# A two-block transformer kernel: the context's projections and attention computed beside the experts, and the experts' second matrices in one buffer, requested by ScalarE

## The chip, the cores and the metric

The kernel runs on one core of one Trainium2 chip. The metric is the device time of one execution in microseconds (us); the time of a kernel is the median of its runs.

## The reference

All data is float32. The input has 512 tokens (D = 1024) and, for the second block, 256 context tokens. The first block is a mixer with two kinds of attention, a layer of 32 experts (two per token) and a gated side input. The second block has two layers; in its first (grouped attention, 16 query heads on 4 key heads of 64) context tokens are queries too:

```python
def hier_moe(x, ...):                      # per expert e, on the tokens routed to it
    hdn = silu(xb @ w1[e]) * (xb @ w3[e])  # w1, w3: 1024 x 512
    return hdn @ w2[e]                     # w2: 512 x 1024, 2 MB each

def gqa_mixer(h, hc, p, cos, sin, with_ctx_out):
    k, v, q, g = split(h @ w_in, ...)      # w_in: 1024 x (256 k, 256 v, 1024 q, 1024 g)
    proj_c = hc @ w_in                     # context: k, v, q, g as well
    k_all, v_all = concat([kc, k]), concat([vc, v])
    o = attend(q, k_all, v_all)            # 512 queries over 768 keys
    y = (o * silu(g)) @ w_out
    oc = attend(qc, kc, vc)                # 256 context queries over the 256 context keys
    yc = (oc * silu(gc)) @ w_out
```

`hc` is the normalised and modulated context. It depends on the inputs alone, not on the first block. q and k are normalised per head and, for the 512 tokens, rotated.

## The kernel before

The program has two blocks, `first_layer` and `second_layers`, with a barrier between them. The rows of a tensor lie on 128 partitions, so the 512 tokens are tiles t = 0 to 3 and the context is tiles 4 and 5. Each engine has its own list of instructions in an order written out by hand; semaphores (`s[...]`) tie them together. An engine that waits holds up everything behind it on its list. DMAs are asked for by SyncE (`sp`), mostly; each engine that asks has a queue of its own.

**The experts.** A loop over e = 0 to 30 (`STATIC` = 31) is unrolled. Every expert takes at most 64 tokens; a loop with a number of passes known only at run time (the "over" loop) does expert 31 and whatever exceeds 64. For each expert PE computes, in this order: the first product of e (`first_product(p1, w1b[p])`), the transposes of the hidden rows of e - 1 (`hidden`), the third matrix's product of e, the transposes of the next expert's rows (`turn_rows`), and the second product of e - 1 (`second`). ScalarE applies silu (L1175) and evicts the second product, scaled by the gates (`outputs`, L1169); VectorE multiplies and copies; GpSimd gathers rows and scatters results. Each of the three matrices (2 MB) has two buffers, used in turn. SyncE asks for them in the order w1, w3, w2 of expert e; it waits for w1's buffer on `h1`, for w3's on `h3`, and for w2's on `y`, the second product of e - 2. Beside the experts PE, ScalarE and VectorE do small jobs at fixed values of e: the modulation rows, tables, the lists for the over loop, and, at e = 20 to 29, the norm of the side input and of the context, whose transposed and modulated tiles are `ctx_in`. At the end of the block SyncE asks for the first six pieces (1 MB each) of `l0_w_in`.

**The second layers.** PE's list begins with the projection of the context (units `("c", n, t)`: three chunks of 512 columns, two tiles, 8 products each), then the context's gates (`("cg", j)`), transposes of `hx` (`("p", t)`) that wait for the sum with the experts' output `y`, the side gate, and the projections of the tokens. All large products are recorded on L1872, transposes on L1880. The attention (`class Attention`, object `gqa`) goes over 8 pairs of heads; for each it has a list of units (pair, tile, first key tile, last key tile, output group, column). Per step n PE computes the scores of unit n + 1 (L327) in one PSUM buffer, the transposes of the next pair's queries and keys if due (L312, `turn_step`), the transposes of the weights of unit n (L339), and the values of unit n - 1 (L353). VectorE takes the maximum (L443), ScalarE the exponential (L526). After it come the output products and the second layer with its own attention (`mla`) of the same class.

## Time and profile before

| | us |
|---|---|
| three timed runs | 2036.48, 2024.63, 2036.65 |
| their median | 2036.48 |
| the profiled execution | 2025.51 |
| its span, first to last instruction | 2023.7 |
| PE busy | 1790.9 (88%) |
| VectorE busy | 732.0 (36%) |
| ScalarE busy | 521.1 (26%) |
| granted TensorE clock, mean | 0.97 |
| bytes moved by DMA | 333.45 MB |

The profile is of one execution. Durations of matmuls are modelled at their ends, so that a busy PE isn't PE at its peak; a product of float32 with 512 columns is recorded as two instructions. The share of busy time is an average over stages with different limits, so a stage has to be read by itself.

### The profile page before, as it was taken

The page shows a single profiled execution, that of the slowest core. Times are in us where ns is not written, and L with a number is a line of the kernel's source. Part 1 is how long each engine was busy: PE and PEld are TensorE (multiplying, and loading weights), DVE is VectorE, ACT ScalarE, POOL GpSimd, SP SyncE. Part 2 cuts the span into 40 slices and gives each one's busy share as a digit, 9 for nine tenths or more (in the row PEclk, how much of TensorE's full clock was granted, in tenths as well). Part 3 has the DMA queues.
Part 4 walks back from the last instruction along what each step waited for, and adds up shares of the span by engine and source line. Part 5 has one row for each costly group of instructions (what it writes and reads, how often), then busy time and mean ns, then how long its engine had stood idle before and what let it go on. Part 6 is the DMA issues. An engine that isn't in the chain of part 4 may idle for free.

```text
span 2023.7 us, 24040 instructions
## 1 busy us (share of the span) xinstructions
PE 1790.9 (88%) x9628; PEld 1007.5 (50%) x9628; DVE 732.0 (36%) x1432; ACT 521.1 (26%) x1102; POOL 152.0 (8%) x202
## 2 busy tenths in 40 slices
PE   8999878978887778875999998888998999699998
PEld 3333455544444444443564445666545544467663
DVE  2333675231131111121213264666333225555542
ACT  2111575210000001110223123445211233234330
POOL 2110000001111111111000130000000000100000
PEclk9999999989999899998999999999998999899999
DMA  7655946269999999998522220000200011000001
GB/s 264 216 182 182 161 73 132 111 259 384 421 421 420 420 421 421 421 420 359 207 85 83 83 83 1 1 1 1 97 0 31 21 57 63 21 1 1 1 22 42
DMA packets 91951, 333.45 MB, mean 165 GB/s; under 512 B 10112, under 2 KB 26624, under 8 KB 64832
## 3 DMA queue, kind: packets, MB, share of 16 engines
q1 hardware_dynamic: 81536, 310.56, 42.1%
q0 software_dynamic: 5200, 17.04, 2.1%
q10 hardware_dynamic: 5104, 4.30, 0.7%
q8 instruction: 77, 1.26, 0.3%
q14 instruction: 34, 0.28, 0.1%
HBM read 317.58 MB, written 14.30 MB: 164 GB/s over the span
## 4 chain that ended last, share of the span: by engine, by line
PE 42%; ACT 6%; DVE 2%; issue 2%; POOL 1%; ACTq 0%; DVEq 0%; POOLq 0%
PE tail_ps L1872 27%; PE tail_ps L327 7%; ACT arena L526 5%; PE tail_ps L339 3%; PE tail_ps L353 2%; PE tail_ps L312 1%; PE tail_ps L1880 1%; POOL extra L2409 1%; DVE tail_small L443 0%; PE tail_ps L373 0%; DVE arena L2368 0%; DVE side L208 0%; DVE arena L208 0%; DVE arena L2369 0%; ACT arena L208 0%
## 5 line engine op out<-in xcount | busy, mean ns | idle before, releaser
L1000 PE MATMUL mix_ps<-arena 128*64 128x256 f32 x2048 | 253.5, 404 | 94.4 <-issue 60.9
L1000 PEld LDWEIGHTS mix_ps<-arena 128*64 128x64 f32 x2048 | 163.1, 145 | 183.6 <-issue 88.9
L1872 PE MATMUL tail_ps<-arena 128*128 128x512 f32 x504 | 219.7, 592 | 0.1
L443 DVE TENSOR_REDUCE tail_small<-tail_ps 128x1 f32<-128x768 f32 (+1 forms) x160 | 128.7, 846 | 150.8 <-PE tail_ps L327 150.8
L888 PE MATMUL mix_ps<-arena,side 128*128 128x512 f32 x384 | 175.5, 610 | 1.4 <-DVE side L1217 1.4
L1872 PEld LDWEIGHTS tail_ps<-arena 128*128 128x128 f32 x504 | 95.1, 190 | 115.2 <-issue 114.7
L526 ACT ACTIVATE arena<-tail_ps,tail_small 128x768 f32<-128x768 f32 (+1 forms) x160 | 128.6, 813 | 3.7 <-DVE tail_small L443 3.7
L888 PEld LDWEIGHTS mix_ps<-arena,side 128*128 128x128 f32 x384 | 72.3, 194 | 103.6 <-issue 85.4
L1872 PE MATMUL tail_ps<-arena,side 128*128 128x512 f32 (+2 forms) x320 | 122.1, 543 | 0.0
L1012 PE MATMUL mix_ps<-arena 128*64 128x512 f32 x512 | 116.9, 598 | 2.3 <-issue 1.8
L339 PE MATMUL tail_ps<-first,arena 128*128 128x128 f32 x832 | 107.3, 277 | 1.2 <-ACT arena L526 0.4
L339 PEld LDWEIGHTS tail_ps<-first,arena 128*128 128x128 f32 x832 | 92.3, 141 | 19.5 <-issue 16.0
L327 PE MATMUL tail_ps<-side,arena 96*128 96x512 f32 (+1 forms) x256 | 92.1, 503 | 8.8 <-ACT arena L526 8.1
L1399 DVE COPY arena<-mix_ps 128x256 f32<-128x256 f32 x31 | 13.2, 424 | 220.3 <-PE mix_ps L1005 219.6
L1169 ACT ACTIVATE arena<-mix_ps,mix_small 128x512 f32<-128x512 f32 x31 | 21.3, 687 | 274.5 <-PE mix_ps L1012 274.5
L1872 PEld LDWEIGHTS tail_ps<-arena,side 128*128 128x128 f32 x320 | 62.3, 196 | 57.1 <-issue 45.4
L327 PE MATMUL tail_ps<-side 64*128 64x256 f32 (+1 forms) x320 | 61.2, 492 | 27.7 <-ACT arena L526 26.6
L1872 PE MATMUL tail_ps<-side,arena 128*128 128x512 f32 x192 | 83.9, 592 | 0.0
L327 PEld LDWEIGHTS tail_ps<-side,arena 96*128 96x128 f32 x256 | 46.5, 191 | 48.8 <-issue 35.2
L1872 PE MATMUL tail_ps<-arena,extra 128*128 128x512 f32 (+1 forms) x128 | 51.3, 561 | 16.1 <-PEq L164 16.1
L1012 PEld LDWEIGHTS mix_ps<-arena 128*64 128x64 f32 x512 | 34.4, 136 | 60.8 <-issue 57.3
L1574 POOL DMA_INDIRECT expert_out<-arena,mix_indices x31 | 30.6, 987 | 424.5 <-ACT arena L1169 417.4
(344 smaller groups left out, 2178.6 us busy)
## 6 DMA issues: line engine op xcount, KB each, us to landing
arena<-in_w SPq DMA_DIRECT2D x96, 2048.0 KB, 18.1
arena<-in_l_w_in SPq DMA_DIRECT2D x22, 1024.0 KB, 7.4
arena<-in_l_w_mod SPq DMA_DIRECT2D x16, 1024.0 KB, 5.0
arena<-in_w_in SPq DMA_DIRECT2D x12, 1024.0 KB, 9.3
arena<-in_l_w_mod SPq DMA_DIRECT2D x16, 512.0 KB, 4.6
residual<-bias_blocks SPq DMA_DIRECT2D x32, 224.0 KB, 13.0
arena<-in_l_w_out SPq DMA_DIRECT2D x6, 1024.0 KB, 5.2
arena<-in_w_out SPq DMA_DIRECT2D x4, 1024.0 KB, 14.7
```

The costliest lines, as they stand in the source:

```text
L312: ins = pe.transpose(Tp[0:rows, bank, z * P:(z + 1) * P], src, m["ident"])
L327: ins = pe.matmul(self.scores_of(n, x)[:, a * P:e * P], q, k, start=True, stop=True)
L339: ins = pe.transpose(Tp[:, bank, z * P:(z + 1) * P], pr[:, n % self.PRB, x, kt * P:(kt + 1) * P], m["ident"])
L353: ins = pe.matmul(O[x * self.dv:(x + 1) * self.dv, oc * P:(oc + 1) * P], self.value_of(g, x, lo + kt), weight, start=(kt == 0), stop=(kt = ...
L443: dve.tensor_reduce(nm[:, b, x:x + 1], self.scores_of(n, x), AX.X, ALU.max, negate=True).then_inc(s["maxed"], 1)
L526: act.activation(pr[:, b, x, 0:k], in_, ACT.Exp, bias=nm[:, b, x:x + 1], scale=scale, accum_out=sm[:, og_b, z, x:x + 1]).then_inc(s["exped ...
L888: last = pe.matmul(ps[:, u % 4], oT[:, k, t * P:(t + 1) * P], weights.slot(W_IN[n, k // 4], 4, 512)[:, k % 4], start=(k == 0), stop=(k == ...
L1000: last = pe.matmul(out[h * CAP:(h + 1) * CAP, 0:H2], x, wb[:, k, h * H2:(h + 1) * H2], start=(k == 0), stop=(k == DK - 1))
L1012: last = pe.matmul(py[h * CAP:(h + 1) * CAP, :], x, wb[:, f, h * 512:(h + 1) * 512], start=(f == 0), stop=(f == FK - 1))
L1169: act.activation(yb[:, e % 2], py, ACT.Copy, scale=gate_w[:, e:e + 1]).then_inc(s["y_out"], 1)
L1574: pool.indirect_dma_start(out=y_rows, out_offset=bass.IndirectOffsetOnAxis(ap=index[:, 1, e:e + 1], axis=0), in_=yb[:, e % 2], in_offset=N ...
L1872: last = pe.matmul(out, lhs(k), rhs(k), start=(k == 0), stop=(k == K - 1))
```

## The change

It has three parts.

1. **The second matrices.** w2 has one buffer, `w2b`. SyncE asks for that of expert 0; ScalarE asks for the one of expert e on its own queue, right after it has evicted the second product of e - 1. In the over loop SyncE waits for all 31 second products before it asks.
2. **The context beside the experts.** The norms at e = 20 to 29 move to e = 1 to 11. At e = 12 to 23 PE does one half unit of the context's k, v, q projection per expert (`context_product`, four products of 512 columns), with weights that come in six pieces of 1 MB into one buffer, asked for by SyncE between the experts' matrices. ScalarE copies the results out and squares them, VectorE normalises (e = 15 to 25). From e = 24 (`C_FIRST`) on, three steps per expert (`context_step`) compute the attention of the 256 context queries over the 256 context keys, in 16 units of two heads by one tile; the buffers lie in SBUF that w2's second buffer and the lists had.
3. **The second layers.** The three chunks `("c", ...)` are gone and the gates come first; the `gqa` object has four units per pair instead of six; the context's gate is multiplied by VectorE (`gate_context`); norms and rotations cover the four token tiles alone.

```diff
-    w2b = [view(proj_w, 8192, D_EXPERT // P, D), view(work, 4096, D_EXPERT // P, D)]
+    w2b = view(proj_w, 8192, D_EXPERT // P, D)
...
-            expert(0, "w2")
-            expert(1, "w2")
+            sp.dma_start(runs(w2b), A["w2"][0].rearrange("(a p j) n -> p a (j n)", a=2, p=P)).then_inc(s["w2"], 16)
...
             for e in range(2, STATIC):
-                for which in ("w1", "w3", "w2"):
-                    expert(e, which)
-                if e == 14:
-                    sp.wait_ge(s["over_indexed"], 1)
+                expert(e, "w1")
+                if e == 2:
+                    sp.wait_ge(s["side_ev"], 2 * XT)
                     sp.dma_start(side_gain, A["g_ple"]).then_inc(s["side_gain"], 16)
+                expert(e, "w3")
+                if e in range(13, 25, 2):
+
+                    i = (e - 13) // 2
+                    sp.wait_ge(*((s["c_mm"], 2 * i) if i else (s["over_indexed"], 1)))
+                    sp.dma_start(piece, src_c[:, 4 * (i % 2):4 * (i % 2) + 4, 512 * (i // 2):512 * (i // 2 + 1)]).then_inc(s["c_in"], 16)
             sp.wait_ge(s["over_indexed"], 1)
             p = STATIC % 2
             with sp.Fori(0, sp.value_load(trips_over, min_val=1, max_val=OVER + 1)) as i:
                 e = sp.value_load(experts_over[:, ds(i, 1)], min_val=0, max_val=N_EXPERTS - 1)
...
+            for n, free in enumerate(("h1", "h3")):
...
-                pe.wait_ge(s["w2"][e % 2], 16 * (e // 2 + 1))
...
+                pe.wait_ge(s["w2"], 16 * (e + 1))
...
+            def context_product(i):
+
+                n, z, t = i // 4, i // 2 % 2, i % 2
+                pe.wait_ge(s["c_in"], 16 * (i // 2 + 1))
+                if i == 0:
+                    pe.wait_ge(s["ctx_gained"], 2)
+                if z == 0 and n:
+                    pe.wait_ge(s["c_ev"], 2 * (n - 1) + t + 1)
+                for k in range(4):
+                    last = pe.matmul(ps[:, 5 + t], ctx_in[:, t, 4 * z + k], piece[:, k], start=(z == 0 and k == 0), stop=(z == 1 and k == 3))
+                last.then_inc(s["c_mm"], 1)
+
+            def context_step(i):
+
+                u, v, w = i - 2, i - 3, (i - 5) // 2
+                if 0 <= u < C_UNITS:
+                    p, t = u // 2, u % 2
+                    pe.wait_ge(s["qk_taken"], qk_after(p))
+                    pe.wait_ge(*((s["ctx_exped"], 2 * u) if u else (s["c_ev"], 6)))
+                    for x in range(2):
+                        last = pe.matmul(ps[:, 5, 256 * x:256 * (x + 1)], qTc[p % 2][:, x, t * P:(t + 1) * P], kTc[p // 2 % 2], start=True, stop=True)
+                    last.then_inc(s["ctx_scored"], 1)
+                if i % 2 == 0 and i < C_UNITS:
+                    p = i // 2
+                    pe.wait_ge(s["c_normed"], 6 if p < 4 else 9)
+                    pe.wait_ge(s["c_ev"], 6)
+                    if p >= 3:
+
+                        pe.wait_ge(s["ctx_o"], p - 2)
+                    if p:
+                        pe.wait_ge(s["qk_taken"], qk_after(p - 1))
+                    for t in range(2):
+                        for x in range(2):
+                            last = pe.transpose(ps[0:64, 6, x * CTX + t * P:x * CTX + (t + 1) * P], cproj[:, t, 512 + p * P + 64 * x:576 + p * P + 64 * x], m["ident"])
+                    if p % 2 == 0:
+                        for t in range(2):
+                            last = pe.matmul(ps[64:128, 6, t * P:(t + 1) * P], cproj[:, t, 32 * p:32 * p + 64], m["ident"], start=True, stop=True)
+                    last.then_inc(s["qk_turned"], 1)
+                if i % 2 and 0 <= w < 8:
+                    pe.wait_ge(s["ctx_taken"], 2 * w + 2)
+                    pe.wait_ge(s["qk_taken"], qk_after(min(w + 2, 7)))
+                    g = w // 2
+                    for t in range(2):
+                        for kt in range(2):
+                            for x in range(2):
+                                last = pe.matmul(ps[64 * x:64 * x + 64, 6, t * P:(t + 1) * P], cproj[:, kt, 256 + 64 * g:256 + 64 * (g + 1)],
+                                                 pTc[t][:, 2 * x + kt], start=(kt == 0), stop=(kt == 1))
+                    last.then_inc(s["ctx_pv"], 1)
+                if 0 <= v < C_UNITS:
+                    pe.wait_ge(s["ctx_scaled"], v + 1)
+                    pe.wait_ge(*((s["ctx_taken"], v) if v else (s["over_indexed"], 1)))
+                    for x in range(2):
+                        for kt in range(2):
+                            last = pe.transpose(ps[:, 7, (2 * x + kt) * P:(2 * x + kt + 1) * P], pr_c[:, v % 2, x, kt * P:(kt + 1) * P], m["ident"])
+                    last.then_inc(s["ctx_weights"], 1)
...
+                if e >= C_FIRST:
+                    context_step(3 * (e - C_FIRST))
                 pe.wait_ge(s["w3"][p], 16 * (e // 2 + 1))
                 if e:
                     pe.wait_ge(s["hid"], e)
@@ -1045,21 +1118,26 @@
                 if e + 1 < STATIC:
 
                     turn_rows(xg[:, 1 - p], s["got"][1 - p], 16 * ((e + 1) // 2 + 1), s["xg_turned"])
+                if e >= C_FIRST:
+                    context_step(3 * (e - C_FIRST) + 1)
                 if e:
                     second(e - 1)
+                if e >= C_FIRST:
+                    context_step(3 * (e - C_FIRST) + 2)
+                if e in range(12, 24):
+                    context_product(e - 12)
...
+            def take_context(i):
+
+                n, t = i // 2, i % 2
+                H = 4 if n == 0 else 8
+                act.wait_ge(s["c_mm"], 4 * n + t + 3)
+                act.activation(cproj[:, t, 512 * n:512 * (n + 1)], ps[:, 5 + t], ACT.Copy).then_inc(s["c_ev"], 1)
+                act.wait_ge(s["c_ev"], i + 1)
+                if i:
+                    act.wait_ge(s["c_normed"], 3 * n + 1 if t else 3 * n - 1)
+                act.activation(sq_c[:, 0:64 * H], cproj[:, t, 512 * n:512 * n + 64 * H], ACT.Square).then_inc(s["own_squared"], 1)
+
+            def context_step(i):
+                u = i - 2
+                if 0 <= u < C_UNITS:
+                    act.wait_ge(s["ctx_maxed"], u + 1)
+                    if u >= 2:
+                        act.wait_ge(s["ctx_weights"], u - 1)
+                    for x in range(2):
+                        act.activation(pr_c[:, u % 2, x], ps[:, 5, 256 * x:256 * (x + 1)], ACT.Exp, bias=nm_c[:, u % 2, x:x + 1], scale=1.0,
+                                       accum_out=sm_c[:, u % 2, x:x + 1]).then_inc(s["ctx_exped"], 1)
+                if i % 2 == 0 and i < C_UNITS:
+                    p = i // 2
+                    act.wait_ge(s["qk_turned"], p + 1)
+                    act.activation(qTc[p % 2], ps[0:64, 6].rearrange("p (x q) -> p x q", x=2), ACT.Copy).then_inc(s["qk_taken"], 1)
+                    if p % 2 == 0:
+                        act.activation(kTc[p // 2 % 2], ps[64:128, 6, 0:256], ACT.Copy).then_inc(s["qk_taken"], 1)
...
-                    act.wait_ge(s["over_indexed"], 1)
-                if e in range(20, 24):
-                    if e > 20:
-                        act.wait_ge(s["own_squared"], e - 20)
-                    act.activation(own, view(side, 0, XT, D)[:, e - 20], ACT.Square, accum_out=ss_s[:, e - 20:e - 19]).then_inc(s["own_squared"], 1)
-                if e in (24, 25):
+                    act.dma_start(w2b.rearrange("p (a j) n -> p a (j n)", a=2), A["w2"][e].rearrange("(a p j) n -> p a (j n)", a=2, p=P)).then_inc(s["w2"], 16)
+                if e >= C_FIRST:
+                    context_step(3 * (e - C_FIRST) + 2)
...
+            def context_step(i):
+                u, v, w = i - 2, i - 3, (i - 5) // 2
+                if 0 <= u < C_UNITS:
+                    dve.wait_ge(s["ctx_scored"], u + 1)
+                    dve.tensor_reduce(nm_c[:, u % 2], ps[:, 5].rearrange("p (x k) -> p x k", x=2), AX.X, ALU.max, negate=True).then_inc(s["ctx_maxed"], 1)
+                if i % 2 and 0 <= w < 8:
+                    dve.wait_ge(s["ctx_pv"], w + 1)
+
+                    dve.tensor_copy(cproj[:, :, 512 + w * P:512 + (w + 1) * P], ps[:, 6, 0:256].rearrange("p (t q) -> p t q", t=CT)).then_inc(s["ctx_o"], 1)
+                if 0 <= v < C_UNITS:
+                    dve.wait_ge(s["ctx_weights"], v + 1)
+                    if v >= 2:
+                        dve.wait_ge(s["ctx_pv"], v // 2)
+                    dve.tensor_copy(pTc[v % 2].rearrange("p k q -> p (k q)"), ps[:, 7]).then_inc(s["ctx_taken"], 1)
+                if 0 <= u < C_UNITS:
+                    dve.wait_ge(s["ctx_exped"], 2 * u + 2)
+                    chain(dve.reciprocal(rc_c[:, u % 2], sm_c[:, u % 2]))
+                    dve.tensor_tensor(pr_c[:, u % 2], pr_c[:, u % 2], rc_c[:, u % 2].unsqueeze(2).to_broadcast([P, 2, CTX]), ALU.mult).then_inc(s["ctx_scaled"], 1)
...
-        pieces = [(q_of[a:e], P, [qT[:, p % 2, a * P:e * P]]) for a, e in ((0, 4), (4, AT))]
+        pieces = [(q_of[0:XT], P, [qT[:, p % 2, 0:XT * P]])]
...
-                    [(p, t, 0, AT, 2 * p, t) if t < XT else (p, t, XT, AT, 2 * p + 1, t - XT) for p in range(8) for t in range(AT)], 2, 1,
+                    [(p, t, 0, AT, p, t) for p in range(8) for t in range(XT)], 2, 1,
...
-            for n in range(3):
-                arrived("c", n)
-                for t in (4, 5):
-                    product(start(("c", n, t)), lambda k: hcT[:, t - 4, k], weights_of(2 * n), range(DK)).then_inc(s["mm"], 1)
             for j in range(DK):
                 if j % 4 == 0:
                     arrived("cg", j // 4)
                 product(start(("cg", j))[:, 0:CTX], lambda k: weights_of(2 * (j // 4))(k)[:, j % 4 * P:(j % 4 + 1) * P], lambda k: hcT[:, :, k], range(DK)).then_inc(s["mm"], 1)
-                if j < XT:
-                    pe.wait_ge(s["added_y"], j + 1)
-                    turn(("p", j), cut(hx[:, j]), DK)
+                t = {3: 0, 4: 1, 6: 2, 7: 3}.get(j)
+                if t is not None:
+                    pe.wait_ge(s["added_y"], t + 1)
+                    turn(("p", t), cut(hx[:, t]), DK)
...
+            def gate_context(j):
+
+                dve.wait_ge(*emptied(("cg", j)))
+                dve.tensor_tensor(gT_c[:, j].rearrange("p (t q) -> p t q", t=CT), gT_c[:, j].rearrange("p (t q) -> p t q", t=CT),
+                                  proj[:, XT:AT, 512 + j * P:512 + (j + 1) * P], ALU.mult).then_inc(s["gated_c"], 1)
```

## Rows read from the trace of the kernel before

**Rows 1.** The page's slices of 50.6 us: tenths of the DMA engines' time.
```profile
DMA  7655946269999999998522220000200011000001
```

**Rows 2.** Windows: stretch, length, busy PE, PEld, DVE, ACT, POOL; clock, DMA share, GB/s.
```profile
450.00:460.00 10.00, 10.00 (x74) 5.29 (x72) 2.81 (x12) 0.69 (x1) 1.11 (x2) 1.00 0.45 154
...
500.00:900.00 400.00, 317.30 (x2134) 177.03 (x2132) 66.69 (x170) 37.85 (x67) 48.94 (x50) 0.96 1.01 420
```

**Rows 3.** Timeline of PE, one expert: start, busy us, what, idle time before.
```profile
702.49 5.32 PE L1000 MATMUL mix_ps<-arena 128*64 128x256 f32 x32 [2.55 <-issue]
...
712.46 3.65 PE L1012 MATMUL mix_ps<-arena 128*64 128x512 f32 x16
```

**Rows 4.** Timeline of ScalarE: evictions of the second product, seven experts apart.
```profile
813.31 0.69 ACT L1169 ACTIVATE arena<-mix_ps,mix_small 128x512 f32<-128x512 f32 x1 [9.57 <-PE mix_ps L1012]
...
926.80 0.69 ACT L1169 ACTIVATE arena<-mix_ps,mix_small 128x512 f32<-128x512 f32 x1 [8.58 <-PE mix_ps L1012]
```

**Rows 5.** Timeline of PE, two successive first products while weights lay ready.
```profile
445.60 3.67 PE L1000 MATMUL mix_ps<-arena 128*64 128x256 f32 x32 [0.78 <-DVE arena L1392]
...
458.09 3.67 PE L1000 MATMUL mix_ps<-arena 128*64 128x256 f32 x32
```

**Rows 6.** Groups by line, PE, 961 to 1010 us: busy, mean ns, idle before.
```profile
L1872 PE MATMUL tail_ps<-arena,extra 128*128 128x512 f32 x96 | 43.2, 613 | 16.1 <-PEq L164 16.1
```

**Rows 7.** Chain that ended last, gqa attention: start, us, what.
```profile
1235.43 1.58 PE tail_ps L327 x8
...
1261.03 1.56 PE tail_ps L327 x8
...
1265.69 1.56 PE tail_ps L327 x8
...
1270.35 1.56 PE tail_ps L327 x8
...
1288.31 1.56 PE tail_ps L327 x8
...
1314.27 1.56 PE tail_ps L327 x8
...
1449.03 41.44 PE tail_ps L1872 x96
```

**Rows 8.** Timeline of the same attention: a short unit's operations on three engines.
```profile
1258.06 0.76 DVE L443 TENSOR_REDUCE tail_small<-tail_ps 128x1 f32<-128x256 f32 x2 [1.17 <-PE tail_ps L327]
...
1258.68 0.60 PE L339 MATMUL tail_ps<-first,arena 128*128 128x128 f32 x4
...
1259.21 1.53 PE L353 MATMUL tail_ps<-arena 128*64 128x128 f32 x24
...
1259.87 0.47 ACT L526 ACTIVATE arena<-tail_ps,tail_small 128x256 f32<-128x256 f32 x1
```

**Rows 9.** Chain that ended last, the second layer's attention (mla).
```profile
1777.16 2.85 PE tail_ps L327 x8
...
1782.95 2.85 PE tail_ps L327 x8
...
1789.11 2.36 PE tail_ps L327 x6
...
1816.33 2.36 PE tail_ps L327 x6
```

**Rows 10.** DMA issues: source, queue, count, KB each, median us to landing.
```profile
arena<-in_l_w_out SPq DMA_DIRECT2D x6, 1024.0 KB, 5.2
```

**Rows 11.** DMA issues of the first 30 us, ScalarE's queue, in order of issue.
```profile
params<-in_params ACTq DMA_DIRECT2D x1, 439.0 KB, 6.7
...
consts<-in_consts ACTq DMA_DIRECT2D x1, 1181.5 KB, 10.9
```

**Rows 12.** Timeline of ScalarE's queue at the start.
```profile
7.86 0.46 ACTq L1099 DMA_DIRECT2D consts<-in_consts  x1
```

**Rows 13.** Window, columns as in rows 2.
```profile
10.00:15.00 5.00, 5.00 (x15) 2.53 (x14) 0.00 (x0) 0.00 (x0) 0.00 (x0) 1.00 1.04 410
```

203 lines of the change are left out of this document (116 added, 87 removed).

## The prediction

> **What bounds the kernel now.** I read the page's slices first: the DMA engines are at nine tenths from about 450 to 950 us and nearly idle afterwards [rows 1]. So there are two regimes, the experts and the second layers, and a move from one to the other has a different price in each. The windows put it in numbers: from 500 to 900 us the DMA share is 1.01 at 420 GB/s, while PE is busy for 317 of 400 us [rows 2]. The timeline of one expert shows who waits: PE is idle for 2.55 us, then needs 5.32 us for the first product, and later 3.65 us for the product with the second matrix [rows 3]. Evictions seven experts apart are 113.5 us apart [rows 4]: a cycle of 16.2 us. Where the weights already lay in SBUF, the same first product took 3.67 us and two starts were 12.49 us apart, a small turn of modulation rows (0.6) among it [rows 5]: PE needs 11.9 us per expert. The cycle is that of the weights, and PE has 16.2 - 11.9 = 4.3 us of cover in each. From 961 us on PE is the chain: the context's three projection chunks take 96 instructions at its head [rows 6], and the stretch from the first scores of the second layer's attention (1235.43) to the output products (1449.03) is 213.6 us [rows 7], a loop of scores, maximum and exponential.
>
> **Removed from the tail: the projections.** Six units of 8 products, 96 instructions. They were busy 43.2 us [rows 6]; the same count runs in 41.44 us elsewhere [rows 7], and the slow first few will now fall on the gate products. That is -41.4 us, all on PE's own chain. The turns of hx, which wait for the sums of y, move behind gate products 3, 4, 6 and 7, and so keep gate products ahead of them where the projections were; I expect 0 to 3 us of waiting, taken as 0.
>
> **Removed from the tail: context queries.** Before, a pair of heads has 4 units over 768 keys and 2 over 256. Scores of full units are 4.66 us apart (1261.03, 1265.69, 1270.35); the first full units of three pairs in a row start at 1261.03, 1288.31 and 1314.27: 27.3 us for a pair beside which keys are turned too, 26.0 without [rows 7]. Now there are 32 full units: 32 x 4.66 = 149.1 us. The turn of the next pair no longer lies beside short units but in the third full one. A turn of queries alone puts four transposes (0.6 us [rows 8]) ahead of the weights that ScalarE must empty before its exponential: 0.5 us, four times. With keys it is 1.3 more (27.3 against 26.0): 1.8 us, three times. Together 7.4, and 4.5 for the last unit's weights, values and division, which are exposed. 161.0 against 213.6 is -52.6 us; the last unit is now a long one, later by 1: -51.6. Bounds: turns at nothing, -60; turns as in the other attention, whose pairs have four units with six pieces to turn and start 27.22 us apart, where its units alone, 5.79 apart, would take 23.2 [rows 9], so 4 us each: -31. One piece or three are nearer to my figure than to six.
>
> **Added to the experts: the pieces.** Six loads of 1.05 MB, 6.29 MB at 420 GB/s [rows 2]: +15.0 us, because here nothing hides a byte. At the end of the stage the old loads of these weights cost nothing: they landed behind the barrier. Bounds: 0 (if the stage had idle DMA time where they fall) and 15. SyncE waits for a product before it asks for the next piece; queued behind that wait is the first matrix of an expert whose buffer isn't free sooner anyway.
>
> **Added: twelve products of four, experts 12 to 23.** 8 instructions of 0.43 us (41.44 / 96 [rows 7]), 3.45 us each. The cycle there is 16.2 + 1.25 = 17.4 us by DMA; PE needs 11.9 + 3.45 = 15.4, and 17.0 with the slow first product of [rows 3]. Nothing; if that cover is gone, up to 0.8 us x 12 = 10.
>
> **Added: the context's attention, experts 24 to 30.** On PE: 16 scores; both heads now lie on partitions 0 to 63, so I take the unpacked price, a third (256 of 768 columns) of the 2.85 us of the other attention's scores [rows 9], 0.95 each: 15.2. Sixteen times four transposes at 0.6, 9.6; eight value products of 16 instructions at 1.1 (24 take 1.53), 8.8; eight query turns at 0.6 and four key turns at 0.5, 6.8 [rows 8]. Together 40.4 us. Seven cycles took 113.5 us; free-running PE would take 7 x 11.9 = 83.3, so 30.2 are cover and +10.2 us stick out. Stalls: from the scores of a step to the transposes of its weights lie one expert product (3.6) and some 3 us of the step's own work, 6.7 us. The chain in between is scores 0.95, maximum 0.8, two exponentials 1.0 with their sums [rows 8], inverse and scaling some 0.9, and gaps: about 4.5. Taken as covered. Bounds: 0 to +33 for all of it.
>
> **Moved: the second matrices.** Before, SyncE asks for them when the product two experts back has read them, and its wait on that product also holds back the first and third matrices behind it. Now ScalarE asks once the product just before is evicted, into the one buffer. The loop is: product 3.65, eviction 0.76 with its wait [rows 3, 4], transfer. In a cycle of 16.2 this leaves 11.8 us. A lone 1 MB lands 5.2 us after its issue [rows 10], so 2.7 us are fixed and 2.1 MB need 7.7. Beside a full SyncE queue ScalarE's share is visible once, at the start: 439 and 1181.5 KB on its queue, the second issued at 7.86 us and landed 10.9 later [rows 11, 12], at 18.8, while the engines moved 410 GB/s [rows 13]. From the first one's issue, 0.4 us earlier, that is 11.3 us for 1.66 MB; less 2 us fixed, 178 GB/s. At this throughout, 2.1 MB need 11.8, the loop 3.65 + 0.76 + 2.7 + 11.8 = 18.9 us. But then SyncE's queue would run dry for 2.7 us in each cycle, as it has only 4.2 MB there and two buffers for each; its dry time falls into the transfer, which then has all engines. With some 7 of 9 us contended it fits the 16.2. I take +0.3 us in ten cycles ahead of the pieces, +3, nothing later, where cycles are longer. At the start the wait on y no longer blocks the fourth expert's matrices: of the 5.5 us of idle DMA between 450 and 460 us [rows 2] I take back 1, since one second matrix is no longer loaded ahead: +2 in sum, bounds -5 and +53 (18.9 in every cycle: 2.7 x 10 + 1.5 x 12 + 1.2 x 7).
>
> The Trainium skill ("DMA: Bandwidth & Descriptors", Queues, rings and completion order) says that each DMA engine goes round the queues that have work, a packet at a time. Halves of 420 would give 10.0 us of transfer and a loop of 17.1, where the one row that shows a share gives 18.9 (178 of 410 is 43%); the sum above needs neither. Its page "Trainium Kernel Development and Optimization" (Best Practices) says to double-buffer so that DMA overlaps compute, and this change takes a buffer away; by that rule the cycle would be the loop's, which is the first rival below.
>
> Everything else (norms, squares, the gate multiplication on DVE) is on engines that are mostly idle; that the context rows' output products start before the attention's end shortens nothing, since PE is dense there.
>
> **Sum** against the profiled run, 2025.5 us (span 2023.7): -41.4 - 51.6 + 15.0 + 10.2 + 2 = -65.8, so 1959.7. Two of the three timed runs lie 11 us above the profiled one, one does not; for a median I add half of that: 1965.
>
> **Rivals.**
> 1. *The one buffer sets the cycle.* For it: 178 GB/s in the only row with two full queues. Against: SyncE can't keep the engines full in a longer cycle. At one more us in 22 cycles, 1987; at 18.9 everywhere, 2016. Chance 0.12.
> 2. *It does so with three queues.* GpSimd's gathers and scatters share the engines too. If ScalarE gets a third, 140 GB/s, the transfer takes 15.0 us and the loop 22.1: 5.9 x 10 + 4.7 x 12 + 4.4 x 7 = 146 us, 2109: slower. It decides from a loop of about 19.6 us (a share of 168 GB/s in every cycle), which eats the whole gain. Against: the gathers are 0.5 MB in a cycle. Chance 0.03.
> 3. *PE stands in the context steps.* PE waits in order for two other engines, each bound to its own order around the expert. 1.5 us in each of 20 steps is +30: 1995. For it: ScalarE must alternate between exponentials and the experts' function; against: the 2.2 us of margin above. Chance 0.13.
> 4. *Turns as dear as in the other attention*: 1986. Chance 0.10.
> 5. *It doesn't add what I count*: pieces and steps fill idle time: 1940. Chance 0.05.
> My own sum, 0.57, with a range of 1948 to 1982.
>
> Range 1938 to 2000: it leaves out rival 2, the far half of 1 and parts of 3. A difference of 1% (20 us) is what a measurement here can tell from none. Faster by over 1% (under 2016): all but rival 2 and the end of rival 1, 0.93; same 0.03; slower 0.04.
>
> **What would show it.** The wait that PE had ahead of the first product moves ahead of the second matrix's; cycles are 16.2 to 16.5 us before expert 12, 17.4 to 23, 17.5 to 18 afterwards. Rival 1 shows 17.2 or more before expert 12 and a DMA share under 0.97 there. Rival 3 shows PE idle inside the steps. In the tail: gates as the first products, attention in 161 us, pairs about 19.7 us apart. I would be wrong above all where a cycle of experts 2 to 11 isn't the DMA engines' any more.

## The result and the profile after

The changed kernel takes 2014.63 us (median of 20 runs, 2006.88 to 2025.43), the one before 2029.43 us (20 runs, 2024.63 to 2036.65). The ratio is 0.9927 (95% interval 0.9913 to 0.9940): 15 us faster, where 66 were forecast. The time lies outside the range (1938 to 2000, with 1965 as the forecast), and in the class to which the forecast gave 0.03.

The profiled executions are 2020.8 us (span 2018.7) and 2025.5 us (span 2023.7). ScalarE's evictions of the second product y(e) cut both at the same places. In the changed kernel (timeline of ScalarE, first, 11th, 23rd, 30th and 31st eviction):

```profile
468.93 0.69 ACT L1247 ACTIVATE arena<-mix_ps,mix_small 128x512 f32<-128x512 f32 x1 [7.92 <-PE mix_ps L1027]
...
644.21 0.69 ACT L1247 ACTIVATE arena<-mix_ps,mix_small 128x512 f32<-128x512 f32 x1 [6.88 <-PE mix_ps L1027]
...
868.76 0.69 ACT L1247 ACTIVATE arena<-mix_ps,mix_small 128x512 f32<-128x512 f32 x1 [13.44 <-PE mix_ps L1027]
...
996.38 0.69 ACT L1247 ACTIVATE arena<-mix_ps,mix_small 128x512 f32<-128x512 f32 x1 [8.40 <-PE mix_ps L1027]
...
1009.95 0.69 ACT L1247 ACTIVATE arena<-mix_ps,mix_small 128x512 f32<-128x512 f32 x1 [12.89 <-PE mix_ps L1027]
```

| stretch | before | after | difference | forecast |
|---|---|---|---|---|
| start to y(0) | 457.6 | 468.9 | +11.3 | 0 |
| y(0) to y(10) | 158.5 | 175.3 | +16.8 | +2 |
| y(10) to y(22), pieces and products | 197.2 | 224.5 | +27.3 | +15 |
| y(22) to y(29), steps | 113.5 | 127.6 | +14.1 | +10.2 |
| y(29) to y(30) | 4.7 | 13.6 | +8.9 | 0 |
| over block and barrier | 30.3 | 29.3 | -0.9 | 0 |
| second part to the attention's first scores | 273.7 | 233.4 | -40.3 | -41.4 |
| attention to the output products | 213.6 | 171.3 | -42.3 | -51.6 |
| rest | 574.7 | 574.7 | 0 | 0 |

The sum is -5.0, up to rounding. The 11.3 us at the start lie in code that the change doesn't touch (the granted clock from 400 to 430 us was 0.77, against 0.93 before; the last section shows two executions of one code that differ by as much); without them it is -16.3, which fits the medians' -14.8. So the tail gave nearly what was forecast, and the experts cost 67 us in place of 27.

The page's groups (before, then changed) say where PE waits: ahead of the second product now, where it had waited ahead of the first product. They also say that the second product itself got slower, 145.2 us for the same 512 instructions where it had been 116.9.

```profile
L1000 PE MATMUL mix_ps<-arena 128*64 128x256 f32 x2048 | 253.5, 404 | 94.4 <-issue 60.9
...
L1012 PE MATMUL mix_ps<-arena 128*64 128x512 f32 x512 | 116.9, 598 | 2.3 <-issue 1.8
```
```profile
L1015 PE MATMUL mix_ps<-arena 128*64 128x256 f32 x2048 | 238.1, 386 | 2.5 <-DVE arena L1510 2.5
...
L1027 PE MATMUL mix_ps<-arena 128*64 128x512 f32 x512 | 145.2, 719 | 66.9 <-DMA arena<-in_w 66.3
```

Two cycles in a row, in the timeline, and the same two as windows (columns as in [rows 2]):

```profile
504.31 0.38 ACTq L1300 DMA_DIRECT2D arena<-in_w  x1
...
519.64 5.34 PE L1027 MATMUL mix_ps<-arena 128*64 128x512 f32 x16 [6.48 <-DMA arena<-in_w]
...
525.04 0.37 ACTq L1300 DMA_DIRECT2D arena<-in_w  x1
...
534.29 3.65 PE L1027 MATMUL mix_ps<-arena 128*64 128x512 f32 x16
...
538.00 0.37 ACTq L1300 DMA_DIRECT2D arena<-in_w  x1
```

```profile
480.00:920.00 440.00, 382.98 (x2314) 192.18 (x2316) 97.49 (x240) 64.79 (x119) 47.60 (x48) 0.91 0.98 395
504.30:525.00 20.70, 14.22 (x91) 7.11 (x91) 2.91 (x11) 2.11 (x4) 1.96 (x2) 0.84 1.00 416
525.00:538.00 13.00, 13.00 (x89) 6.68 (x90) 2.23 (x4) 2.12 (x5) 1.96 (x2) 1.00 0.93 355
```

The DMA issues of those two stretches, with the time to landing:

```profile
arena<-in_w ACTq DMA_DIRECT2D x1, 2048.0 KB, 15.3
arena<-in_w ACTq DMA_DIRECT2D x1, 2048.0 KB, 8.6
```

Up to y(10) the cycles alternate. In the long one w2 lands 15.3 us after its request and PE stands 6.48 us for it. In the short one it lands after 8.6 us, but PE needs 13.0 us for its own work and can't be any faster. At the start of the short cycle the four buffers of w1 and w3 are full, so SyncE has nothing to ask for until PE has read one, and the DMA engines fall to 355 GB/s over the cycle. These two cycles make 16.9 us on average, the ten from y(0) to y(10) 17.5, where the cycle before was 16.2.

The long cycle is long for a second reason: the clock. The second product as windows, in the long cycle and in the short one:

```profile
519.64:524.98 5.34, 5.33 (x17) 1.50 (x17) 0.00 (x0) 0.00 (x0) 0.00 (x0) 0.68 0.97 403
534.29:537.94 3.65, 3.65 (x18) 1.12 (x17) 0.69 (x1) 0.00 (x0) 0.00 (x0) 1.00 1.00 422
```

Behind the wait of 6.48 us the granted clock was 0.68 in the mean of the product, so in part at 1.2 GHz, the lower of the two levels, and the product took 5.34 us. Where PE hadn't waited it stayed at 2.4 GHz and took 3.65. The next w2 is asked for only behind this product, so what it loses goes round the loop. In the five long cycles up to y(10) it took 5.99, 5.34, 5.59, 5.09 and 6.60 us, in the short ones 3.65: 10.4 of the 16.8 us that this stretch lost.

And the last second matrix is asked for behind y(29), at 996.38 us, with nothing left to cover it:

```profile
1004.79 5.11 PE L1027 MATMUL mix_ps<-arena 128*64 128x512 f32 x16 [8.03 <-DMA arena<-in_w]
```

### The profile page after: what moved, and what is told of

Same layout as the page of the kernel before. It is cut to its first block and busy times, and to the rows that moved or that the text cites. A ratio compares the mean times of both kernels' runs of the same rounds, so it can differ in the third digit from the quotient of the medians.

```text
span 2018.7 us, 24057 instructions
## 1 busy us (share of the span) xinstructions
PE 1821.2 (90%) x9644; PEld 1007.6 (50%) x9644; DVE 753.6 (37%) x1471; ACT 540.1 (27%) x1110; POOL 148.2 (7%) x194
## 5 line engine op out<-in xcount | busy, mean ns | idle before, releaser
L1015 PE MATMUL mix_ps<-arena 128*64 128x256 f32 x2048 | 238.1, 386 | 2.5 <-DVE arena L1510 2.5
L1027 PE MATMUL mix_ps<-arena 128*64 128x512 f32 x512 | 145.2, 719 | 66.9 <-DMA arena<-in_w 66.3
L1015 PEld LDWEIGHTS mix_ps<-arena 128*64 128x64 f32 x2048 | 143.3, 138 | 89.1 <-issue 20.2
L903 PE MATMUL mix_ps<-arena,side 128*128 128x512 f32 x384 | 175.3, 609 | 1.4 <-DVE side L1335 1.4
L443 DVE TENSOR_REDUCE tail_small<-tail_ps 128x1 f32<-128x768 f32 x128 | 116.6, 953 | 137.7 <-PE tail_ps L327 137.7
L526 ACT ACTIVATE arena<-tail_ps,tail_small 128x768 f32<-128x768 f32 x128 | 113.8, 899 | 3.7 <-DVE tail_small L443 3.7
L1027 PEld LDWEIGHTS mix_ps<-arena 128*64 128x64 f32 x512 | 40.6, 164 | 147.6 <-issue 77.2
L339 PE MATMUL tail_ps<-first,arena 128*128 128x128 f32 x768 | 98.2, 277 | 9.5 <-DVE side L208 8.3
L339 PEld LDWEIGHTS tail_ps<-first,arena 128*128 128x128 f32 x768 | 85.9, 142 | 24.5 <-issue 15.8
L2031 PEld LDWEIGHTS tail_ps<-side,arena 128*128 128x128 f32 x192 | 36.5, 190 | 45.9 <-issue 45.9
L2031 PE MATMUL tail_ps<-extra,arena 128*128 128x256 f32 (+1 forms) x160 | 45.7, 444 | 15.1 <-PEq L164 15.1
## 6 DMA issues: line engine op xcount, KB each, us to landing
residual<-bias_blocks SPq DMA_DIRECT2D x32, 224.0 KB, 10.1
```

Of the source, the lines that this page charges most:

```text
L339: ins = pe.transpose(Tp[:, bank, z * P:(z + 1) * P], pr[:, n % self.PRB, x, kt * P:(kt + 1) * P], m["ident"])
L443: dve.tensor_reduce(nm[:, b, x:x + 1], self.scores_of(n, x), AX.X, ALU.max, negate=True).then_inc(s["maxed"], 1)
L526: act.activation(pr[:, b, x, 0:k], in_, ACT.Exp, bias=nm[:, b, x:x + 1], scale=scale, accum_out=sm[:, og_b, z, x:x + 1]).then_inc(s["exped ...
L903: last = pe.matmul(ps[:, u % 4], oT[:, k, t * P:(t + 1) * P], weights.slot(W_IN[n, k // 4], 4, 512)[:, k % 4], start=(k == 0), stop=(k == ...
L1015: last = pe.matmul(out[h * CAP:(h + 1) * CAP, 0:H2], x, wb[:, k, h * H2:(h + 1) * H2], start=(k == 0), stop=(k == DK - 1))
L1027: last = pe.matmul(py[h * CAP:(h + 1) * CAP, :], x, wb[:, f, h * 512:(h + 1) * 512], start=(f == 0), stop=(f == FK - 1))
```

## The experiments

All ratios are to the kernel before. The stretches are read from each run's profile, by the same evictions as above, in us.

| kernel | ratio (95%) | y(0)-y(10) | y(10)-y(22) | y(22)-y(29) | y(29)-y(30) | y(0)-y(30) |
|---|---|---|---|---|---|---|
| before | 1 | 158.5 | 197.2 | 113.5 | 4.7 | 473.8 |
| one_sp | 1.0059 (1.0034-1.0084) | 160.9 | 196.6 | 113.2 | 14.0 | 484.7 |
| two_act | 0.9989 (0.9972-1.0005) | 153.3 | 199.1 | 109.7 | 8.7 | 470.9 |
| one_act | 1.0280 (1.0234-1.0326) | 177.1 | 212.1 | 121.4 | 18.5 | 529.1 |
| act_held_2 | 1.0332 (1.0288-1.0375) | 184.4 | 219.4 | 129.8 | 19.7 | 553.3 |
| after | 0.9927 (0.9913-0.9940) | 175.3 | 224.5 | 127.6 | 13.6 | 541.0 |
| after_sp | 1.0159 (1.0131-1.0186) | 161.2 | 283.9 | 127.6 | 14.7 | 587.4 |
| after_sp_piece | 0.9788 (0.9748-0.9829) | 161.3 | 211.2 | 127.6 | 14.8 | 514.9 |
| no_steps | 0.9895 (0.9852-0.9938) | 176.4 | 223.4 | 119.1 | 14.8 | 533.7 |
| ring5 | 0.9819 (0.9777-0.9861) | 155.5 | 238.5 | 127.6 | 4.6 | 526.3 |
| ring5_piece | 0.9731 (0.9691-0.9770) | 154.6 | 212.7 | 127.6 | 4.6 | 499.6 |
| spread | 0.9652 (0.9620-0.9684) | 155.8 | 211.5 | 115.0 | 5.5 | 487.8 |
| spread_turn | 0.9627 (0.9602-0.9652) | 155.7 | 211.8 | 115.0 | 5.5 | 487.9 |

**The second matrices in the kernel before: buffer and queue apart.** one_act does the change's first part alone.

```
-    w2 of expert e: SyncE, behind w1(e), w3(e), into w2b[e % 2] when y >= e - 1
+    outputs(e - 1)
+    act.dma_start(w2b[0], A["w2"][e]).then_inc(s["w2"], 16)
```

> The kernel before with one part of the change alone: a single buffer for the second matrices, which ScalarE requests on its own queue behind each eviction of y. Theory 1, the one buffer costs: the matrix can be asked for only at y(e-1) and for part of each second cycle nothing is left to move, so the 30 cycles take 17.2 to 17.5 us in place of 16.2 (+30 to +40 us) and the last matrix lies bare at the end (+5 to +9 us): ratio 1.017 to 1.024. Theory 2, not the buffer but the second queue: the same time here. Theory 3, the products and attention steps beside the experts cost what is missing, the buffer nothing: ratio 1.00 to 1.005.

one_sp has the one buffer and keeps SyncE's queue; the loop asks in the order of use.

```
-    for which in ("w1", "w3", "w2"): expert(e, which)
+    expert(e, "w1"); expert(e, "w3")
+    sp.wait_ge(s["y"], e - 1); sp.dma_start(w2b[0], A["w2"][e - 1])
```

> The kernel before with the single buffer, but the second matrices stay on SyncE's queue, asked for in the order of use (w1(e), w3(e), w2(e-1)). Theory 1 (the buffer): as dear as with ScalarE's queue, 1.015 to 1.03, since the matrix can be asked for no earlier and the next first matrix now stands behind it. Theory 2 (two queues share the engines badly): the cycles are back at 16.2 us and only the last matrix at the end costs, ratio 1.00 to 1.005. Theory 3: 1.00.

two_act has both buffers and ScalarE's queue.

```
     outputs(e - 1)
+    act.dma_start(w2b[(e + 1) % 2], A["w2"][e + 1])
```

> The other half of the change to the second matrices alone: the kernel before with both its buffers, but ScalarE asks for w2(e+1) on its own queue behind the eviction of y(e-1), the moment at which the buffer comes free. Theory A (the loss needs both, one buffer and a transfer that shares the engines with matrices needed later): with a whole expert of slack the slow landing of w2 (12 to 15 us) is hidden, ratio 0.995 to 1.005. Theory B (two queues as such waste the engines): 1.01 to 1.03.

The windows of the three, one_sp, two_act, one_act:

```profile
480.00:920.00 440.00, 340.67 (x2358) 189.21 (x2360) 74.04 (x189) 39.69 (x71) 52.81 (x54) 0.99 1.01 420
```
```profile
480.00:920.00 440.00, 363.31 (x2392) 196.63 (x2390) 76.33 (x190) 40.34 (x72) 51.91 (x53) 0.91 1.01 421
```
```profile
480.00:920.00 440.00, 342.87 (x2189) 172.89 (x2191) 66.48 (x182) 36.02 (x66) 48.95 (x50) 0.88 0.97 390
```

One buffer alone leaves the transfers at 420 GB/s and costs 11 us, of which 9.3 are the bare last matrix; the ratio, 1.0059, lies just above theory 2's range. The second queue alone leaves them at 421 and costs nothing. Together they cost 55 us, more than theory 1 had expected, and the rate falls to 390. Neither "the one buffer" nor "two queues as such" holds: it takes both.

act_held and act_held_2 asked whether it is the order: in one_act SyncE asks for w1(e + 2) 8 to 19 us ahead of w2(e) (from 500 to 540 us). The edit, as act_held_2 has it:

```
                 if e >= 2:
                     sp.wait_ge(s[dict(w1="h1", w3="h3")[which]], e - 1)
+                    if e > 2:
+                        sp.wait_ge(s["y_out"], e - 2)
```

> As one_act (the kernel before, one buffer, second matrices on ScalarE's queue), but SyncE holds w1(e) and w3(e) back until y(e-2) is evicted, the moment at which ScalarE asks for w2(e-1): still two queues and one buffer, but the matrices that are needed later are no longer asked for first. Theory A, the order: w2 shares the engines with matrices asked for 8 us earlier and needed an expert later; held back, the 30 cycles fall from 17.6 us to 16.2 to 16.5 and the ratio from 1.028 to 1.006 to 1.012. Theory B, two queues as such waste the engines: the ratio stays at 1.02 to 1.03. Theory C, holding back starves the queue: over 1.03.

act_held had `y_out >= e - 1` as its only wait, one expert too long. Ratio 1.1784, DMA share 0.60: the starved queue of theory C, which says nothing on the order.

> act_held with its hold set right: w1(e) and w3(e) are now held back until y(e-3) is evicted, as SyncE's own order in one_sp had them (act_held held them one expert longer and starved the queue, which says nothing of the order). Theory A: w2(e-2) and w1(e), w3(e) are asked for at the same moment, no later matrix is ahead of the second one; the 30 cycles fall from 17.6 us to 16.2 to 16.7, ratio 1.006 to 1.012 in place of 1.028. Theory B: 1.02 or more.

It came out at 1.0332, not at 1.006 to 1.012: theory A in this form is wrong. one_sp and act_held_2 ask for the same matrices at nearly the same moments, and differ in the queue of w2. The landing of w2, for three requests of one_sp (at 594, 643 and 659 us) and four in a row of act_held_2 (from 701 us on):

```profile
arena<-in_w SPq DMA_DIRECT2D x1, 2048.0 KB, 12.5
arena<-in_w SPq DMA_DIRECT2D x1, 2048.0 KB, 12.4
arena<-in_w SPq DMA_DIRECT2D x1, 2048.0 KB, 12.9
```
```profile
arena<-in_w ACTq DMA_DIRECT2D x1, 2048.0 KB, 11.5
arena<-in_w ACTq DMA_DIRECT2D x1, 2048.0 KB, 15.7
arena<-in_w ACTq DMA_DIRECT2D x1, 2048.0 KB, 11.1
arena<-in_w ACTq DMA_DIRECT2D x1, 2048.0 KB, 16.4
```

Behind what SyncE had asked for before and ahead of what it asks for next, w2 lands in 12.4 to 12.9 us each time, and 12.4 + 3.65 is the cycle of 16.2. On a queue of its own it shares the engines with whatever SyncE's queue then holds, and its landing swings between 11 and 16. With two buffers a late landing has an expert of slack; with one it is PE's time at once, and in the changed kernel an early one isn't paid back, as PE has 12 to 13 us of its own work in a cycle. The Trainium skill ("DMA: Bandwidth & Descriptors", Queues, rings and completion order) says that SP and ACT each own one row of queues and that an engine goes round the rows for which it has work; the landings agree, while no run here shows the packets themselves. The Trainium skill ("Trainium Kernel Development and Optimization", Best Practices) also says to double-buffer; one_sp shows that rule broken for 1.5 us in the 29 cycles to y(29), with the transfers at 420 GB/s all the while, and for 9.3 us in the last one.

The swing isn't the whole joint cost; most of it is the clock behind the waits. The group of the second product in one_act, one_sp and after_sp_piece (below):

```profile
L1016 PE MATMUL mix_ps<-arena 128*64 128x512 f32 x512 | 159.2, 779 | 127.6 <-DMA arena<-in_w 126.9 <-issue 0.7
```
```profile
L1018 PE MATMUL mix_ps<-arena 128*64 128x512 f32 x512 | 123.3, 625 | 53.2 <-DMA arena<-in_w 53.2
```
```profile
L1032 PE MATMUL mix_ps<-arena 128*64 128x512 f32 x512 | 124.3, 630 | 28.9 <-DMA arena<-in_w 26.3 <-issue 2.5
```

In one_sp PE stands for w2 as well, but mostly for some 1.6 us at a time, and from 480 to 920 us the granted clock is 0.99; in one_act it is 0.88. So of the 44.4 us between one_act and one_sp from y(0) to y(30) some 36 are second products that ran slower behind a longer wait. act_held_2 (161.2 us in this group) shows both terms side by side, as PE waits for w2 in each of its 30 cycles: their mean of 18.4 us is 13.3 from the request to the product and 5.1 of product, where one_sp has 12.3 (in the 28 in which it waits) and 3.8. In two_act the granted clock falls too (0.91), but there the waits and the slow products are the first ones (6.19 us at 659.12, behind a wait of 6.41), the second is busy for 118.5 us in all, and w2, with its second buffer, is in time all the same. No run holds the clock, so what the swing of the landings would cost at 2.4 GHz is not shown.

**The same in the changed kernel.** after_sp is the changed kernel with one_sp's order of requests.

```
     expert(e, "w1"); expert(e, "w3")
+    sp.wait_ge(s["y"], e - 1); sp.dma_start(w2b, A["w2"][e - 1])
     if e in range(13, 25, 2): ... sp.dma_start(piece, ...)
```

> The changed kernel with its one buffer, but the second matrices asked for by SyncE in the order of use (w1(e), w3(e), w2(e-1)); all else as changed. Theory A or B (ScalarE's queue costs, by order or as such): evictions of y(0) to y(10) come within 161 us in place of 175, the stretch of y(10) to y(22) falls from 224.5 to 205 to 215 us, y(29) to y(30) stays at 14 us; ratio 0.975 to 0.985. Theory of the one buffer (already weakened): no change, 0.993.

The first stretch did as theory A or B said (161.2), but the second rose to 283.9. A piece now stood behind w2(e - 1) and its wait for y, and so was asked for an expert after its buffer had been read:

```profile
731.50 0.47 SPq L857 DMA_DIRECT2D arena<-in_l_w_in  x1
...
744.85 6.56 PE L1060 MATMUL mix_ps<-arena,extra 128*128 128x512 f32 x8 [13.80 <-DMA arena<-in_l_w_in]
```

In the changed kernel, where SyncE doesn't wait for y, PE stood for no piece: its waits from 644 to 869 us are all for w2. after_sp_piece puts the piece in its own place in the order of use, ahead of w1(e).

```
+    if e in range(13, 25, 2): ... sp.dma_start(piece, ...)
     expert(e, "w1")
     expert(e, "w3")
     sp.wait_ge(s["y"], e - 1); sp.dma_start(w2b, A["w2"][e - 1])
-    if e in range(13, 25, 2): ... sp.dma_start(piece, ...)
```

> The changed kernel with its one buffer for the second matrices, asked for by SyncE in the order of use (as after_sp), and with the pieces of context's projection asked for ahead of w1(e), in their place in the order of use, too (as ring5_piece). after_sp alone fell to 1.016, because a piece now stood behind a request that waits for y and TensorE then stood 13.8 us for it. If the joint cost of one buffer and a second queue is what the forecast missed in the changed kernel as in the one before: y(0) to y(10) 161 us, y(10) to y(22) 210 to 216 (224.5 as changed), y(22) to y(29) 127.6 unchanged (TensorE sets it), y(29) to y(30) 13 to 15; ratio 0.978 to 0.985 in place of 0.993. If in the changed kernel another cost is hidden behind it: over 0.99.

All four stretches and the ratio are within what was expected. From y(0) to y(30) it is 26.1 us under the changed kernel: that is the joint cost there. The second product's group fell from 145.2 to 124.3 us, so some 21 of the 26.1 stand in it. What is left over the kernel before is 2.8 and 10.1 us for the one buffer (first and last stretch), 14.0 for the pieces and 14.1 for the steps.

**Five buffers that any matrix may use.** ring5 keeps the changed kernel's SBUF, but SyncE asks for all 93 matrices in the order of use, number i into buffer i % 5.

```
+    turn_of: w1(e) -> 3e - 1, w3(e) -> 3e, w2(e) -> 3e + 4
+    i = turn_of(which, e); _, of, before = order_of_use[i - 5]
+    sp.wait_ge(s[dict(w1="h1", w3="h3", w2="y")[of]], before + 1)
+    sp.dma_start(five[i % 5], A[which][e]).then_inc(s["five"][i % 5], 16)
```

> The changed kernel with the same five buffers, but any matrix may lie in any of them: SyncE asks for all 93 matrices in the order of use, each into the buffer that was freed five matrices earlier; ScalarE asks for none. Theory 1: queue never runs dry, cycles of experts 0 to 12 are back at 16.2 us (-13 us), those with pieces at 17.4 (-16 us), and the last matrix is covered (-6 to -9 us): ratio to the kernel before 0.975 to 0.982. Theory 2 (one queue in place of two) gives the same here. Theory 3 (PE's added work sets the cycles from expert 12 on): -13 us at most before expert 12, -9 at the end, ratio 0.983 to 0.987.

The ratio is as theory 1 had it, but not by its stretches: the first is back under that of before (155.5), the last as before (4.6), yet the second rose by 14 us. A piece again stands behind four matrices that are needed later:

```profile
619.01 0.47 SPq L857 DMA_DIRECT2D arena<-in_l_w_in  x1
...
645.78 6.64 PE L1060 MATMUL mix_ps<-arena,extra 128*128 128x512 f32 x8 [13.56 <-DMA arena<-in_l_w_in]
```

ring5_piece moves the pieces ahead of w1(e), the same move as in after_sp_piece.

> ring5 with each piece of context's projection asked for two matrices earlier, ahead of w1(e) in place of behind w2(e-1), which is its place in the order of use. In ring5 a piece landed 12 to 27 us after its request, behind up to four matrices needed later, and TensorE stood 4.6 us for it in every second cycle, 13.6 us once. If the pieces' place is what costs: y(10) to y(22) falls from 238.5 us to 209 to 215 and the ratio from 0.982 to 0.968 to 0.972. If the products on TensorE cost it (15.5 us of its work in a cycle): it stays above 230 us and the ratio at 0.98.

212.7 us as expected, and the ratio 0.9731, 0.001 above its range, with its interval across it. The window over this stretch has the transfers at their limit while both products run beside them:

```profile
620.00:810.00 190.00, 171.35 (x1016) 87.37 (x1014) 34.28 (x87) 21.57 (x36) 21.55 (x22) 0.97 1.02 418
```

That is 15.5 us over the kernel before, for six pieces: the forecast's +15.0.

**The attention steps.** no_steps sets `C_UNITS = 0`, which leaves out the context's attention.

> The changed kernel without context's attention steps at experts 24 to 30 (scores, weights and outputs of context's attention are left out on all engines, so its rows carry the queries in their place). Theory 1: the stretch from the eviction of y(22) to that of y(29) falls from 127.6 us to 119 to 122 (7 cycles of 17.2 us), the kernel by 6 to 9 us, ratio to the kernel before 0.988 to 0.990. Theory 3 (the steps cost all that this stretch lost): it falls to 113.5 us and the ratio to 0.985 or 0.986. If the steps hide wholly behind the transfers: no change, 0.9927.

119.1 us, theory 1's figure: of the 14.1 us that the stretch lost, the steps hold 8.5, and without them PE waits for w2 again (8.55 us ahead of the product at 937.49, which then takes 5.31). spread has the same work in another place.

```
-C_FIRST = 24                                # steps 3 (e - 24) + 0, 1, 2
+C_FIRST = 21                                # steps 2 (e - 21) + 0, 1
+PIECE_AT = (12, 13, 15, 16, 18, 19)         # both products of a piece here
```

> ring5_piece with context's work spread out: both products of a piece in one expert (12, 13, 15, 16, 18, 19) in place of one an expert from 12 to 23, and the attention steps two an expert from 21 to 30 in place of three from 24. The sum of TensorE's work is the same, but it stays under the transfers' time in nearly each cycle. If TensorE's work in steps sets the stretch from y(22) to y(29) (18.2 us a cycle, engine never idle, DMA share 0.93 there): that falls from 127.6 us to 113 to 117, and the kernel by 8 to 16 us, ratio 0.965 to 0.969. If the steps cost for another reason (their place, the transfers): the same as ring5_piece, 0.973.

115.0 us, and the ratio 0.9652. The windows of the changed kernel and of spread over the same 90 us:

```profile
870.00:960.00 90.00, 89.00 (x640) 52.96 (x640) 38.55 (x75) 36.15 (x81) 9.52 (x10) 1.00 0.95 365
```
```profile
870.00:960.00 90.00, 88.47 (x651) 51.04 (x649) 30.83 (x59) 29.28 (x61) 9.82 (x10) 1.00 1.00 414
```

PE is full in both. With three steps an expert the transfers wait for it (365 GB/s); with two, both are full, and the seven experts take 16.4 us each in place of 18.2.

**The turns in the tail's attention.** turn_act lets ScalarE empty the turned queries.

```
-self.place(("turn", ..., j), j % 2)
+self.place(("turn", ..., j), (j + turn_by) % 2)     # turn_by = 1 for gqa alone
```

> The changed kernel, in the first attention of the second part, with the turned queries emptied by ScalarE in place of VectorE (keys swapped likewise). If a turn is dear because VectorE empties it behind two maxima and TensorE waits for the bank (1.05 us at 1334.06): a step with a turn of queries falls from 6.1 us to 5.0 to 5.4, the attention's 171.3 us by 5 to 8. If the step is set by TensorE's own work or by VectorE's sum: by under 2 us.

PE's timeline over a step with a turn of queries, in the changed kernel and in turn_act:

```profile
1329.99 1.56 PE L327 MATMUL tail_ps<-side 64*128 64x512 f32 x8
...
1331.98 1.04 PE L339 MATMUL tail_ps<-first,arena 128*128 128x128 f32 x8
1334.06 0.66 PE L339 MATMUL tail_ps<-first,arena 128*128 128x128 f32 x4 [1.05 <-DVE side L208]
...
1336.11 1.56 PE L327 MATMUL tail_ps<-side 64*128 64x512 f32 x8
```
```profile
1332.64 1.56 PE L327 MATMUL tail_ps<-side 64*128 64x512 f32 x8
...
1337.83 1.56 PE L327 MATMUL tail_ps<-side 64*128 64x512 f32 x8 [0.23 <-ACT arena L526]
```

The third set of transposes waits for the bank that holds the turned queries, which VectorE empties only behind two maxima. Emptied by ScalarE, the step is 5.19 us in place of 6.12; one with keys gains 0.15. From the first to the last scores it is 157.7 us in place of 161.8 (one execution, 2020.57 us, no ratio): 4.1, a little less than the 5 to 8 expected. spread_turn joins this to spread.

> spread, and ScalarE empties the turned queries of the attention behind (turn_act's edit, 4.1 us less there from first to last scores). The two lie in different stages: 4 us under spread, ratio 0.963 to 0.967.

1958.79 us, ratio 0.9627, just under its range: the fastest here, and 3% under the changed kernel. The difference to spread by the ratios, 0.25%, is 5 us, inside both intervals; by the profiles the attention gains its 4 us.

## Why the prediction was wrong

**The step that failed: "Moved: the second matrices".** The price was +2 us; it is 39 (26.1 joint, 2.8 and 10.1 for the buffer by itself). Three faults lie in it.
- The loop "product 3.65, eviction 0.76, transfer" has the product at full clock. The forecast had the other price: the product behind a wait took 5.32 us in place of 3.67 [rows 3], and it said itself that this wait would move ahead of the second product. There the slow product holds up the next request. It took 5.1 to 6.6 us in the long cycles: 10.4 us up to y(10), and 28.3 over the whole group (145.2 against 116.9). With 3.65 in each, the ten cycles would have come to 16.5 us (an estimate: 175.3 less 10.4), which is the forecast's 16.2 + 0.3.
- It found the contended landing (2.7 + 11.8 = 14.5 us; measured 15.3 in the long cycles), then let SyncE's dry time "fall into the transfer, which then has all engines". That took the mean of a landing that swings. The dry time comes in the other cycle: w2 landed in 8.6 us there, and PE, not w2, ended it.
- The last second matrix had no term at all. In a loop of e, the term for the last round has to be written down by itself: +8.9.

Rival 1, at 0.12, was the case by its first sign, over 17.2 us a cycle ahead of expert 12 (17.5). Its second, a DMA share under 0.97 there, showed in the short cycles alone (0.93; 0.98 from y(0) to y(10)). Its price of one us in 22 cycles (1987) was near the 26.1 us, but it had neither the last matrix nor the two terms below, nor the clock.

**Pieces, +15.0:** right where nothing is beside them (14.0 and 15.5 in after_sp_piece and ring5_piece). What the forecast said of their queue, that only a matrix "whose buffer isn't free sooner anyway" stands behind them, was half of the question. What stands ahead of a piece cost 26 us in ring5.

**Products, 0:** right, once requests are in order. Rival 5 (all hidden) is out.

**Steps, +10.2:** 14.1. The prices per instruction held: in the timeline of expert 27, scores, values and transposes of a step start 1.05, 1.03 and 0.58 us apart.

```profile
930.33 1.13 PE L1065 MATMUL mix_ps<-arena 64*128 64x256 f32 x4
931.38 1.09 PE L1090 MATMUL mix_ps<-arena 128*64 128x128 f32 x16
932.41 0.66 PE L1098 MATMUL mix_ps<-first,arena 128*128 128x128 f32 x4
932.99 3.67 PE L1015 MATMUL mix_ps<-arena 128*64 128x256 f32 x32
```

What was left out is that the stretch from y(22) also holds the last of the twelve products, 3.5 us: it had been counted as covered by the same 4.3 us of an expert in which the steps' cover was counted. With it the sum is 83.3 + 40.4 + 3.5 = 127.2 us against 127.6; no run moved that product alone. Rival 3 (PE stands in the steps) isn't there.

**Projections, -41.4:** -40.3. **Queries, -51.6:** -42.3. The unit of 4.66 us held. A group of four is 2 x 4.66 + 4.94 + 6.12 (7.39 with keys), where the forecast had 3 x 4.66 + 5.16 (6.46): 1.2 us more in each of six, 7.4. The first group took 21.4 us in place of 19.1, with a granted clock of 0.63 from 1277.16 to 1281.80 (one set of scores took 2.71 us there, behind a wait of 2.92), and the last took 0.3 less than its 24.1: 9.3 in all. The turn was priced by PE's transposes. For queries its price is VectorE's place in the bank ring, as turn_act shows (0.93 of the 1.46 us); for the turns with keys, 2.7 us each, turn_act gained 0.15, and what sets them isn't shown. Rival 4 put this at 4 us a turn, too dear.

In sum: second matrices +37.0, queries +9.3, steps +3.9, projections +1.1, pieces -1.0, barrier -0.9, and 11.3 of the start: 60.8 between the -65.8 forecast and the -5.0 of the profiled executions.

What stays open: why the landing on ScalarE's queue swings from cycle to cycle, even in act_held_2 where all requests come at the same point of each; how much of the joint cost would be left at full clock; and in the changed kernel the joint cost is shown as a whole, not cycle by cycle.

## What to carry to other kernels

One buffer or a queue of its own may each cost little (1.5 us in 29 cycles and nothing here), and the two together be dear (55 us): a transfer that is asked for just in time wants a landing that doesn't swing, so leave it in the one queue, in the order of use, or give it slack. Ask too which product stands behind the new wait: if the next request hangs on it, put it into the loop at what it takes behind a wait (here 5.1 to 6.6 us, not 3.65). A ring of equal buffers that any matrix may take, asked for in the order of use by one engine, did with five buffers what six had done, and each other load has to be asked for in its own place in that order. Don't average a loop whose two sides take turns at being late, and write the last round of a loop down by itself.

## What the runs showed of the hardware

The code up to y(0) is the same in spread and spread_turn, yet y(0) is evicted at 469.66 and 458.29 us. The windows of spread and of spread_turn over the routing:

```profile
380.00:400.00 20.00, 20.00 (x54) 9.23 (x53) 4.88 (x14) 6.07 (x9) 0.00 (x0) 1.00 0.19 79
400.00:430.00 30.00, 30.00 (x130) 21.00 (x129) 15.51 (x58) 7.06 (x12) 0.00 (x0) 0.83 0.41 158
```
```profile
380.00:400.00 20.00, 20.00 (x65) 10.10 (x65) 4.73 (x10) 3.38 (x5) 0.00 (x0) 1.00 0.12 37
400.00:430.00 30.00, 24.60 (x128) 16.43 (x126) 16.38 (x64) 7.95 (x15) 2.11 (x2) 1.00 0.52 201
```

From 380 to 400 us PE was busy without a gap in both; in one the granted clock then was 0.83 in the mean of 30 us, so in part at 1.2 GHz, the lower of its two levels, and in the other it stayed at 2.4. The profiled execution of before had 457.62 and that of the change 468.93: a comparison of two single profiles of this kernel carries about 11 us that belong to no edit.

Also, w2 on ScalarE's queue landed 15.3 us after its request while the engines moved 416 GB/s: less some 2.7 us fixed [rows 10], 2.1 MB in 12.6 us are 166 GB/s by estimate, 40% of all, not half. two_act's trace has no landings for this queue; its ratio, 0.9989, shows no cost.
